# A two-block network on one core: the first input's modulation summed another way, loads held back, and VectorE's side sums at other places

## The reference

```python
c_act = silu(c)                                        # c: (1, 1024)
for i in range(2):
    sh1, sc1, g1, sh2, sc2, g2 = split(c_act @ w_ada[i] + b_ada[i], 6)   # w_ada[i]: 1024 x 6144
    u = x * (1 + sc1) + sh1
    y = gla_mixer(u, ...) if i == 0 else chunk_attention(u, ...)
    x = layer_norm(ALPHA * x + (1 + g1) * y, ...)
    u = x * (1 + sc2) + sh2
    y = squared_relu_mlp(u, ff_w1[i], ff_w2[i])        # width 4096
    x = layer_norm(ALPHA * x + (1 + g2) * y, ...)
# then a hybrid mixer (pooling, indexed sparse attention, gates) and a gated convolution MLP
```

## Time and profile before

| | us |
|---|---|
| median of 3 runs | 1044.97 (1044.95 to 1045.06) |
| profiled execution | 1045.0 |
| its span, first to last instruction | 1043.3 |
| TensorE busy | 1002.4 |
| VectorE busy | 802.8 |
| ScalarE busy | 507.7 |
| GpSimd busy | 70.0 |

### The profile page before, as it was taken

The page is one execution under the profiler, slowest core; times in us unless marked ns, Lnnn a source line. Parts: engine busy times, 40 slices in busy tenths (PEclk is TensorE's granted clock), DMA queues, the critical chain, the costliest instruction groups (busy, mean ns, idle before and its releaser), DMA issues.

```text
span 1043.3 us, 16755 instructions
## 1 busy us (share of the span) xinstructions
PE 1002.4 (96%) x6806; PEld 900.3 (86%) x6806; DVE 802.8 (77%) x1254; ACT 507.7 (49%) x684; POOL 70.0 (7%) x147
## 2 busy tenths in 40 slices
PE   7999989999998999999999999899999999999996
PEld 7987768989997798888989998789988989999995
DVE  4499898998998877668886567767884858777776
ACT  3484435334334655726344443634456456555563
POOL 3101210110010111000100000100000000000000
PEclk9999999999999999999999999999999999999999
DMA  9968765899999474443966655263343435565551
GB/s 348 401 226 303 295 251 206 299 341 356 324 338 332 143 281 154 138 155 123 370 235 203 221 168 177 96 211 122 122 162 121 166 131 188 188 205 192 183 194 68
DMA packets 35180, 227.96 MB, mean 219 GB/s; under 512 B 4224, under 2 KB 4352, under 8 KB 10272
## 3 DMA queue, kind: packets, MB, share of 16 engines
q1 hardware_dynamic: 25232, 167.01, 45.6%
q0 software_dynamic: 9872, 59.89, 15.3%
HBM read 225.82 MB, written 1.06 MB: 217 GB/s over the span
## 4 chain that ended last, share of the span: by engine, by line
PE 66%; DVE 19%; issue 6%; ACT 6%; DMA 2%; POOL 0%; POOLq 0%; DVEq 0%; ACTq 0%
PE ps L450 60%; DVE ada_raw L1517 6%; DVE weight_lo L1501 5%; ACT weight_hi L1072 4%; DVE mlp_relu L1898 1%; DMA ada_raw<-ada 1%; DMA weight_raw<-weights 1%; PE ps L845 1%; DVE dev L1653 1%; DVE dev L1646 1%; PE ps L952 1%; PE ps L835 1%; PE ps L834 0%; DVE act_lo L1590 0%; PE ps L584 0%
## 5 line engine op out<-in xcount | busy, mean ns | idle before, releaser
L1501 DVE TENSOR_TENSOR weight_lo<-weight_raw,weight_hi 128x2048 fp32r<-128x2048 f32 (+2 forms) x192 | 310.0, 1619 | 65.0 <-ACT weight_hi L1072 65.0
L1072 ACT ACTIVATE weight_hi<-weight_raw 128x2048 fp32r<-128x2048 f32 (+2 forms) x168 | 298.7, 1787 | 54.8 <-PE ps L450 42.8
L450 PE MATMUL ps<-act_hi,weight_hi 128*128 128x256 f32 x1336 | 317.5, 281 | 3.3 <-DVE act_lo L1590 1.9
L450 PE MATMUL ps<-act_lo,weight_hi 128*128 128x256 f32 x1336 | 312.4, 277 | 0.0
L450 PEld LDWEIGHTS ps<-act_hi,weight_hi 128*128 128x128 f32 x1336 | 250.2, 187 | 12.7 <-issue 7.7
L450 PEld LDWEIGHTS ps<-act_lo,weight_hi 128*128 128x128 f32 x1336 | 250.3, 187 | 3.2 <-issue 1.0
L450 PE MATMUL ps<-act_hi,weight_lo 128*128 128x256 f32 x1336 | 174.5, 277 | 0.1
L450 PEld LDWEIGHTS ps<-act_hi,weight_lo 128*128 128x128 f32 x1336 | 161.5, 187 | 0.5 <-DVE weight_lo L1501 0.3
L450 PE MATMUL ps<-weight_hi,mlp_hi 128*128 128x512 f32 x256 | 100.6, 393 | 4.6 <-DVE mlp_lo L1904 4.6
L1256 ACT ACTIVATE mlp_hi<-mlp_relu 128x512 fp32r<-128x512 f32 x32 | 20.3, 634 | 169.8 <-DVE mlp_relu L1898 166.3
L450 PE MATMUL ps<-weight_hi,mlp_lo 128*128 128x512 f32 x256 | 100.2, 392 | 0.0
(11 more groups left out here) (320 smaller groups left out, 1323.2 us busy)
## 6 DMA issues: line engine op xcount, KB each, us to landing
weight_raw<-weights SPq DMA_DIRECT2D x144, 1024.0 KB, 5.1
ada_raw<-ada POOLq DMA_DIRECT2D x48, 1024.0 KB, 7.4
weight_raw<-weights SPq DMA_DIRECT2D x23, 512.0 KB, 3.7
row_g<-ln_rows POOLq DMA_DIRECT2D x4, 512.0 KB, 4.3
row_b<-ln_rows POOLq DMA_DIRECT2D x4, 512.0 KB, 5.4
att_bias<-rel_bias POOLq DMA_DIRECT2D x16, 128.0 KB, 3.6
square<-gates POOLq DMA_DIRECT2D x3, 512.0 KB, 4.4
dev<-x_in SPq DMA_DIRECT2D x1, 1024.0 KB, 9.2
```

Of the source, the lines that this page charges most:

```text
L450: return e.matmul(o, a, b, start=start, stop=False, skip_group_check=True)
L1072: e.activation(weight_hi[h][:, 0:size], weight_raw[r][:, 0:size], ACT.Copy).then_inc(hi_full[h], 1)
L1501: ins = e.tensor_tensor(weight_lo[h][:, a + at:b + at], weight_raw[r][:, c], weight_hi[h][:, c].bitcast(F32), ALU.subtract)
```

## The change

Five parts:

1. *First input.* A load now has the 128 features' weights of `sh1` as eight blocks (columns 0 to 1023) and those of `sc1` turned, with features in the partitions (columns 1024 to 2047). TensorE sums all of the shift with 8 matmuls. VectorE sums the scale in one operation with the accumulator. The order on VectorE is now sum, residue of the tile before, modulation of this tile, split of a weight chunk. ScalarE casts weight chunks 1 and 2 one tile later.
2. *Loads.* Ada load 8 waits until load 7 has landed, weight chunk 3 until the eighth sum is made.
3. *Side sums.* VectorE makes two right behind the first input, and in the mixer of the first layer two fewer among its first steps and others at other places. The first MLP has 16 in place of 20, each in front of a block's second `split_lo`. Attention has 8, one in every slot, in place of 4. GpSimd's loads go along.
4. *Between MLP and attention.* Nine filler matmuls around `turn(1, 0)`, the second half's rows are normalized in front of the cast of the held chunk, and TensorE turns them before it waits for that chunk.
5. *Values of the third block's mixer.* TensorE's order is rewritten (`mixer_values`), fillers are split in 6 and 3, and VectorE splits the held chunk behind the second half's input.

```diff
                 else:
+                    if j == N_RAW:
+                        e.wait_ge(ada_used, KT)
...
-                    e.wait_ge(hi_full[(j + c) % N_SPLIT], (j + c) // N_SPLIT + 1)
                     if turn_at and turn_at[1] == 2 * c:
                         turn(turn_at[0], 1)
+                    e.wait_ge(hi_full[(j + c) % N_SPLIT], (j + c) // N_SPLIT + 1)
...
+            def mixer_values(j):
...
+                e.wait_ge(*emptied(W["mv0"]))
+                high(0, 0)
+                low(0, 0)
+                high(0, 1)
+                keep_busy("mv1", 6)
+                turn(3, 1)
+                keep_busy("mv1", 3)
+                high(1, 0)
+                low(1, 0).then_inc(chunk_done, 1)
+                high(1, 1)
+                low(0, 1).then_inc(v_done, 1)
+                low(1, 1).then_inc(chunk_done, 1)
...
-                raw = ada_raw[slot][:, :].rearrange("p (k n) -> p k n", k=KT)
+                raw = ada_raw[slot][:, 0:D].rearrange("p (k n) -> p k n", k=KT)
                 e.wait_ge(ada_full[slot], 16 * (f // N_ADA_RING + 1))
                 if f >= 2:
                     e.wait_ge(u_mods, f - 1)
-                for x in range(2):
-                    c = slice(x * P, (x + 1) * P)
-                    for k in range(U_ROWS, KT):
-                        mm(ps[:, 6 + f % 2, c], raw[:, k, c], c_act[:, k:k + 1].broadcast_to([P, P]),
-                           start=(x == 0 and k == U_ROWS))
-                e.wait_ge(ada_used, f + 1)
-                for x in range(2):
-                    last = mm(ps[:, 6 + f % 2, x * P:(x + 1) * P], ada_acc[:, (2 * f + x) * P:(2 * f + x + 1) * P], ones_sq[:, :])
+                for k in range(KT):
+                    last = mm(ps[:, 6 + f % 2, 0:P], raw[:, k, :], c_act[:, k:k + 1].broadcast_to([P, P]), start=(k == 0))
...
             up_down(0, 0)
+            keep_busy("av0", 5)
             turn(1, 0)
+            keep_busy("av0", 4)
...
-                if k in (1, 3, 5):
-                    split_hi(k // 2)
+                if k in (1, 4, 6):
+                    split_hi((1, 4, 6).index(k))
...
             input_hi_half(1, 0)
+            norm_rows(1, 1, 1)
             split_hi(HELD[1])
-            norm_rows(1, 1, 1)
...
+                def scale_sum(f):
+                    slot = f % N_ADA_RING
+                    raw = ada_raw[slot][:, D:CW]
+                    e.wait_ge(ada_full[slot], 16 * (f // N_ADA_RING + 1))
+                    e.scalar_tensor_tensor(out=raw, in0=raw, scalar=1.0, in1=c_row[:, :], op0=ALU.mult, op1=ALU.mult,
+                                           accum_out=mod(0, 1, f)).then_inc(ada_used, 1)
+
                 def mods_of_tile(f):
                     b = VEC["b_ada"] + f
+                    e.wait_ge(ada_used, f + 1)
+                    e.scalar_tensor_tensor(out=norm_scale[:, 0, f:f + 1], in0=mod(0, 1, f), scalar=1.0,
+                                           in1=vec[:, b + KT:b + KT + 1], op0=ALU.add, op1=ALU.add).then_inc(u_scale, 1)
                     e.wait_ge(u_summed, f + 1)
-                    e.tensor_tensor(mod(0, 0, f), ps[:, 6 + f % 2, 0:1], vec[:, b:b + 1], ALU.add).then_inc(u_shift, 1)
-                    e.wait_ge(u_shift, f + 1)
-                    e.scalar_tensor_tensor(out=norm_scale[:, 0, f:f + 1], in0=ps[:, 6 + f % 2, P:P + 1], scalar=1.0,
-                                           in1=vec[:, b + KT:b + KT + 1], op0=ALU.add, op1=ALU.add).then_inc(u_mods, 1)
+                    e.tensor_tensor(mod(0, 0, f), ps[:, 6 + f % 2, 0:1], vec[:, b:b + 1], ALU.add).then_inc(u_mods, 1)
...
-                e.wait_ge(c_done, 1)
+                e.wait_ge(c_row_in, 1)
                 for f in range(KT):
-                    slot = f % N_ADA_RING
-                    to = ada_acc[:, 2 * f * P:2 * (f + 1) * P]
-                    raw = ada_raw[slot][:, :].rearrange("p (k n) -> p k n", k=KT)
-                    if f:
-                        mods_of_tile(f - 1)
-                    e.wait_ge(ada_full[slot], 16 * (f // N_ADA_RING + 1))
-                    n = own.of(e.tensor_scalar(to, raw[:, 0, :], c_act[:, 0:1], None, ALU.mult))
-                    for k in range(1, U_ROWS):
-                        e.wait_ge(dve_step, n)
-                        ins = e.scalar_tensor_tensor(out=to, in0=raw[:, k, :], scalar=c_act[:, k:k + 1], in1=to,
-                                                     op0=ALU.mult, op1=ALU.add)
-                        if k < U_ROWS - 1:
-                            n = own.of(ins)
-                    ins.then_inc(ada_used, 1)
+                    scale_sum(f)
                     if f:
                         residue(f - 1)
+                    mods_of_tile(f)
                     if f in (2, 5, 7):
                         split_lo((2, 5, 7).index(f))
-                mods_of_tile(KT - 1)
                 residue(KT - 1)
...
             first_input()
 
 
+            ada_chunk()
+            ada_chunk()
...
             split_lo(7)
-            ada_chunk()
             gate_product(0)
             decayed_q(1)
             decayed_k(1)
             split_lo(8)
             gate_product(1)
...
             gate_columns(0)
+            gla_mask(3)
             gated_head(0)
-            gla_mask(3)
+            ada_chunk()
             gla_states(1)
...
             split_lo(15)
+            ada_chunk()
             gated_head(3)
             out_residue(2)
-            ada_chunk()
-
-
             add_bias(0, 3)
-            ada_chunk()
+            add_bias(0, 4)
+
+
             out_residue(3)
             split_lo(J_OUT0 + 3)
-            add_bias(0, 4)
...
-                    if (m, i) in ((0, 4), (0, 13), (1, 8)):
-                        gate_columns(3 if m else 1 + (i == 13))
-                    if m == 1 and 3 <= i < 7:
+                    if (m, i) in ((0, 4), (1, 8)):
+                        gate_columns(2 * m + 1)
+                    if m == 0 or 3 <= i < 7:
+                        ada_chunk()
+                    if m == 0 and i == 4:
                         ada_chunk()
                     split_lo(up_chunk(m, i) + 3)
-                    if m == 0 and i < 4:
-                        ada_chunk()
-                    elif m == 0:
-                        ada_chunk()
-                        if i % 2 == 0 and i < n_blocks - 2:
-                            ada_chunk()
                 last = down_chunk(m, n_blocks - 1)
                 split_lo(last)
                 hidden(n_blocks - 1)
                 if m == 0:
                     add_bias(1, 0, 2)
+                    gate_columns(2)
...
-            input_lo_half(1, 0)
-            ln_second(1)
+            input_lo_half(1, 0, lambda: ln_shift(1, 1))
+            ln_second(1, False)
...
                 split_lo(J_ATT + 6 + slot)
-                if slot < 4:
-                    ada_chunk()
+                ada_chunk()
...
-            split_lo(HELD[3], 0, 2)
             square_root(3, 1)
-            split_lo(HELD[3], 1, 2)
             rms_second(3)
             input_lo_half(3, 1)
+            split_lo(HELD[3])
...
                     if i >= N_ADA_RING:
-                        e.wait_ge(u_summed if i < KT + N_ADA_RING else ada_used, i - N_ADA_RING + 1)
+                        e.wait_ge(ada_used, i - N_ADA_RING + 1)
+                        if i < KT + N_ADA_RING:
+                            e.wait_ge(u_summed, i - N_ADA_RING + 1)
+                    if i == KT:
+                        e.wait_ge(ada_full[(KT - 1) % N_ADA_RING], 16 * ((KT - 1) // N_ADA_RING + 1))
...
+                if h > N_BIAS and h % 2:
                     load_ada()
             mask_bias(ATT_H - 1)
+            load_ada(2)
             for t in range(ST):
                 ln_power(5 + t, t)
             load_ln_rows(3)
-            load_ada(4)
...
-    out = [t[0, :, :, 0:2].reshape(KT, P, 2, KT, P).transpose(3, 1, 0, 2, 4).reshape(KT, P, CW)]
+    shift, scale = t[0, :, :, 0].reshape(KT, P, KT, P), t[0, :, :, 1].reshape(D, KT, P)
+    out = [np.concatenate([shift.transpose(2, 1, 0, 3).reshape(KT, P, D), scale.transpose(1, 2, 0)], 2)]
```

50 lines of the change are left out of this document (32 added, 18 removed).

## The result

The changed kernel takes 1050.35 us in the median (1049.32 to 1051.36, 5 runs), the kernel before 1044.97: ratio 1.0048 (95% interval 1.0031 to 1.0065). It is 5.4 us slower where 7 us less were forecast. Its profiled execution has a span of 1049.0 us, 5.7 more than before.

The account below looks back on a forecast made before the run. TensorE, busy 96% of the span, was taken as the bound through its waits. Terms -2.4 - 0.9 - 6.0 - 0.4 + 5.7 - 3.1 = -7.1 on 1045.0 gave 1037.9, stated 1038.0; range 1032.0 to 1042.5.

Parts of the forecast that it names:

- First input, -2.4: First input: fewer TensorE records per tile bring the gate matmul from 49.60 to 47.1 us; term -2.4 us.
- tile 6 at 31 again: First input: stated sign of a wrong forecast, tile 6 starting at 31 us instead of the forecast 29.2.
- rival (c): First input gains nothing, since loads end its waits; total -4.7 us, 1040.3 us; chance 0.14.
- So the held loads are hidden: First input: chunk 3 goes out about 8 us later but costs nothing; 1.5 us if that cover fails.
- First layer's mixer, -0.9: First layer's mixer: two sums moved into VectorE's idle time gain 2.4 us, head 3 gives some back; term -0.9.
- 1.3 + 0.2: First mixer, head 3: the sum ahead of its gated product costs 1.3 us, the pow beside it 0.2 more.
- The -0.5: First mixer's total instead of -0.9 if the cited rule makes the sum hold head 3's pow 0.6 us, not 0.2.
- First MLP, -6.0: First MLP: fewer sums, placed in VectorE's wait for ScalarE's cast, remove the 4.63 us wait and low clock; -6.0 us.
- Into attention, -0.4: Between first MLP and attention: fillers hidden, the held chunk's cast follows the row scaling, its low half comes earlier; -0.4 us.
- Attention, +5.7: Attention: four more sums lengthen VectorE's slots, delaying softmaxes, turns and the output projections; +5.7 us.
- rival (e): Slower kernel: TensorE's clock falls in attention slot 6 and stays low into the output projections; 1049.4 us; chance 0.05.
- Third mixer's values, -3.1: Third block's mixer values: the second half's turn no longer waits for the held chunk's split; -3.1 us.

Follow-up runs that it names:

- 5: Changed kernel without the held loads, with the mixer's last sum behind head 3's product and attention's four added sums in the first MLP: 1036.05 us, 0.9910.
- 6: Kernel of 5 with the whole first input of the kernel before the change: 1036.58 us, 0.9917.
- 9: Kernel of 5 with weight chunk 0's load waiting for ada load 0's landing, no longer for its sum: 1037.48 us, 0.9925.
- 10: Kernel of 5 with filler matmuls in the first input, 15 behind tile 2's columns and 8 ahead of tile 3's: 1037.48 us, 0.9925.
- 11: Kernel of 5 with VectorE's split of weight chunk 2 ahead of tile 7's modulation again: 1035.88 us, 0.9910.
- 14: Kernel of 11 with the two sums behind the first input, and their loads, moved back into the mixer: 1037.22 us, 0.9909.
- experiment 4: Changed kernel with the four sums of attention slots 4 to 7 made in the first MLP, GpSimd's loads along: 1041.55 us, 0.9957.
- experiment 7: Kernel before with only the new order between first MLP and attention and the rewritten values of the third block's mixer: 1043.68 us, 0.9984.
- 1: Changed kernel with 15 filler matmuls behind tile 2's columns in the first input: 1050.74 us, 1.0047.
- 3: Changed kernel with the first mixer's last sum back behind the gated product of head 3: 1048.51 us, 1.0023.
- 8: Changed kernel with 21 filler matmuls in attention's three gaps, around slots 6 and 7: 1047.31 us, 1.0015.

## Why the prediction was wrong, step by step

- **First input, -2.4: wrong sign, +1.7.** "Its load starts 0.5 us later" was the first slip: the sum needs `c_row`, and it started 1.5 us later. Then I let TensorE run on through a gap of 3.8 us that followed from my own step (tile 2 done early, chunk 0 at 19.5), without asking what its clock does. Tile 3 ended at 25.6, not 22.2, and so the load of tile 6 was released 3.9 us late; it then took 6.2 us where I had 7.0. My sign of being wrong, tile 6 at 31 again, came: 32.27. But to mend these slips gains nothing, as the old and the new form are equal (experiments 5 and 6): with an earlier chunk 0 tiles 4 and 5 wait for their loads (9), with an earlier tile 6 TensorE waits for VectorE at 35 us (10), and a gate matmul 2.2 us earlier is taken back by chunk 5's load (11). So rival (c), which I gave 0.14, is right that nothing is gained; its reason, the loads, is right for tiles 4 and 5 and for chunk 5, but not alone. Of the 1.7 us a good part is scatter: with this same first input other executions have the gate matmul at 50.1 to 50.6.
- **"So the held loads are hidden": wrong.** I compared the load time of chunk 3 with when ScalarE wants it, and it was hidden. The bytes were not: the share of 0.71 came back as 4.0 us at chunk 5, two loads further. I put the term at nothing; without the waits the first state product is 3.6 us earlier and the whole 2.4 us faster.
- **First layer's mixer, -0.9: +4.0.** The waits of 1.2 and 0.7 us behind VectorE lost their old releasers, but one for `gla_k`, by way of chunk 5, took their place (1.6). The step itself, two sums moved into an idle time, is worth its 2.4 or nearly: with the sums moved back (14 against 11) the first state product is 2.1 us later, though chunk 5 is 1.3 us earlier. For head 3 I had 1.3 + 0.2; it cost 2.7, of which 1.2 the delay and 1.5 a clock of 0.57. The low clock is the term that I left out; the 1.3 was right and the 0.2 was not needed, as the power was done before the sum. The rule cited there ("SBUF — State Buffer", "Who interferes with whom", in the Trainium skill), that such a VectorE operation holds off GpSimd's reads, agrees with the trace: the power took 1.58 us beside the sum and 0.71 without it. The -0.5 that I drew from it does not follow, since the longer power ended nobody's wait.
- **First MLP, -6.0: right, -6.5.** The wait for `mlp_lo` and the low clock are gone. The reason was half right: the place fills VectorE's wait for the cast, and whether there are 16 sums or 20 makes no difference (experiment 4).
- **Into attention, -0.4: +0.4**, and 0 in experiment 7. Too small to tell.
- **Attention, +5.7: the waits were 5.7, and the clock 3.2 on top.** That the waits meet the forecast to the tenth is in part luck. The clock is rival (e), to which I gave 0.05. Its argument against ("behind the 1.2 us of the first layer it did not fall") took one gap, and here three lie close together. Of the two waits that I put before turns, slot 7's came (1.8 us for 2.4) and slot 6's did not; in its place stand 1.76 and 1.67 us for ScalarE's copies behind the cast, which I had not looked at. The rule of the Trainium skill ("TensorE: Matmul & The Clock Gate", "What's actually happening"), that the default is the low level and activity releases it, agrees with the trace: means of 0.63 and 0.68 behind the gaps, and 1.00 again from 455 us.
- **Third mixer's values, -3.1: right, -2.8.**

The sum was -7.1 and came out as +5.7. Of the 12.8 us between, 4.1 are the first input, 4.9 the mixer, 3.2 attention's clock, 0.6 the rest. The range had room for costs of one kind at a time; three came together. The steps that failed are thus the held loads put at nothing, the release times of the first input, and the clock behind gaps that the forecast itself had made.

## What to carry to other kernels

Where the transfers' share is near 1 and a load ends the next wait behind a stretch, count bytes and not only release times: here time saved ahead of chunk 5 was worth nothing, and loads held back were paid for later, at a chunk that nobody held. The share alone does not say it: the first MLP ran at 0.96 from 200 to 250 us and its gain was whole, because there VectorE ended the wait. Side work on an engine that is nearly level with TensorE belongs into a wait that the trace shows (here ahead of the second split, behind a cast); 20 sums cost there what 16 do, while four sums in attention's full slots cost 5.7 us of waits. And where a forecast makes gaps on TensorE, price the low clock behind them as a cost that may come: here 3.2 us on 5.7 of waits in attention, 1.5 on 1.2 at head 3.

## What was unexpected of the hardware

- Behind the same gap the clock does not always fall: ahead of the output projection it was low in three executions of five (0.57, 0.70 and 0.72 from 142 to 146 us) and 1.00 in two.
- Behind a gap of 1.76 us in attention the clock stayed at 1.00 (in experiments 1 and 3 it was 0.90 and 0.66 from 425 to 430 us there); behind two of 1.83 and 1.67 us within 5 us it was 0.63 to 0.68 for about 9 us. With 42 filler records in the three gaps it stayed at 1.00, and 3.2 us came back.
- With one and the same first input (the changed kernel and experiments 3, 4 and 8) the gate matmul came at 51.32, 50.56, 50.60 and 50.12 us: where transfers are full, one execution can't show a difference of 1 us.
